# In the seven products of quadrants, VectorE's evacuations stand ahead of the weight splits of the same step

## The reference

```python
def swiglu_ffn(x, w_in, w_out):
    gate, up = jnp.split(x @ w_in, 2, axis=-1)
    return (jax.nn.silu(gate) * up) @ w_out
...
h = h + FFN_RES_WEIGHT * swiglu_ffn(rmsnorm(h, norm_ffn1[l]), ffn1_w_in[l], ffn1_w_out[l])
```

## Time and profile before

| | |
|---|---|
| median of 3 runs | 2157.2 us (2157.14 to 2157.84) |
| profiled execution, its own time | 2157.14 us |
| span of the profiled execution | 2155.3 us |
| TensorE busy | 2140.4 us, 99% of the span |
| VectorE busy | 1561.7 us, 72% |
| ScalarE busy | 891.9 us, 41% |
| granted TensorE clock, mean | 0.998 |

### The profile page before, as it was taken

The page is one execution under the profiler, slowest core; times in us unless marked ns, Lnnn a source line. Parts: engine busy times, 40 slices in busy tenths (PEclk is TensorE's granted clock), DMA queues, the critical chain, the costliest instruction groups (busy, mean ns, idle before and its releaser), DMA issues.

```text
span 2155.3 us, 30597 instructions
## 1 busy us (share of the span) xinstructions
PE 2140.4 (99%) x12718; PEld 1899.4 (88%) x12718; DVE 1561.7 (72%) x1798; ACT 891.9 (41%) x1110; POOL 166.0 (8%) x135
## 2 busy tenths in 40 slices
PE   9999999999999999999999999999999999999998
PEld 7998998888777888998998898998788888998997
DVE  8975976453466548984898897697788768874983
ACT  6532533242233425541445543344572356442443
POOL 0000003610123100000000000000102002000002
PEclk9999999999999999999999999999999999999999
DMA  4332332232222223332242233233222123332231
GB/s 162 108 128 69 108 118 98 98 118 95 81 79 78 80 88 116 108 128 78 99 134 84 79 106 127 79 99 108 88 69 69 50 86 111 99 127 79 98 132 45
DMA packets 59176, 210.39 MB, mean 98 GB/s; under 512 B 6560, under 2 KB 8992, under 8 KB 58784
## 3 DMA queue, kind: packets, MB, share of 16 engines
q1 hardware_dynamic: 58464, 205.30, 28.3%
q0 software_dynamic: 288, 2.62, 0.3%
q10 hardware_dynamic: 288, 0.52, 0.1%
HBM read 206.33 MB, written 2.10 MB: 97 GB/s over the span
## 4 chain that ended last, share of the span: by engine, by line
PE 94%; DVE 4%; ACT 1%; issue 1%; DMA 0%; SPq 0%; DVEq 0%; ACTq 0%
PE accs L672 25%; PE accs L673 25%; PE accs L674 25%; PE mixbs L674 3%; PE mixbs L673 3%; PE mixbs L672 3%; PE mixbs L1240 1%; PE mixbs L1217 1%; DVE w_lo L1834 1%; PE accs L1179 1%; PE accs L1178 1%; PE accs L1177 1%; ACT w_hi L1301 0%; PE mixbs L1059 0%; DVE rstd L1969 0%
## 5 line engine op out<-in xcount | busy, mean ns | idle before, releaser
L1301 ACT ACTIVATE w_hi<-w_raw 128x1024 fp32r<-128x1024 f32 x497 | 515.4, 1054 | 600.6 <-PE accs L674 281.9
L1834 DVE TENSOR_TENSOR w_lo<-w_raw,w_hi 128x1024 fp32r<-128x1024 f32 x497 | 613.7, 1238 | 108.9 <-ACT w_hi L1301 102.6
L672 PE MATMUL accs<-x_hi,w_hi 128*128 128x512 f32 (+1 forms) x1408 | 490.7, 349 | 2.1 <-DVE x_lo L1901 1.8
L674 PE MATMUL accs<-x_hi,w_lo 128*128 128x512 f32 (+1 forms) x1408 | 484.0, 344 | 0.0
L673 PE MATMUL accs<-x_lo,w_hi 128*128 128x512 f32 (+1 forms) x1408 | 483.8, 344 | 0.0
L672 PEld LDWEIGHTS accs<-x_hi,w_hi 128*128 128x128 f32 x1408 | 267.0, 190 | 35.6 <-DVE x_lo L1901 3.1
L674 PEld LDWEIGHTS accs<-x_hi,w_lo 128*128 128x128 f32 x1408 | 266.9, 190 | 32.0
L673 PEld LDWEIGHTS accs<-x_lo,w_hi 128*128 128x128 f32 x1408 | 267.2, 190 | 29.9
L672 PE MATMUL accs<-hid_hi,w_hi 128*128 128x512 f32 (+1 forms) x714 | 275.8, 386 | 0.0
L673 PE MATMUL accs<-hid_lo,w_hi 128*128 128x512 f32 (+1 forms) x714 | 275.7, 386 | 0.0
L674 PE MATMUL accs<-hid_hi,w_lo 128*128 128x512 f32 (+1 forms) x714 | 275.6, 386 | 0.0
(11 more groups left out here) (408 smaller groups left out, 3086.5 us busy)
## 6 DMA issues: line engine op xcount, KB each, us to landing
w_raw<-weights SPq DMA_DIRECT2D x383, 512.0 KB, 3.2
y_t<-h SPq DMA_DIRECT2D x16, 128.0 KB, 1.9
h<-x_t SPq DMA_DIRECT2D x3, 512.0 KB, 6.4
k1c<-const POOLq DMA_DIRECT2D x1, 1536.0 KB, 7.7
k2c<-const POOLq DMA_DIRECT2D x1, 1024.0 KB, 7.7
h<-x_t ACTq DMA_DIRECT2D x2, 256.0 KB, 4.0
w_raw<-weights SPq DMA_DIRECT2D x1, 384.0 KB, 4.8
cst<-const SPq DMA_DIRECT2D x1, 161.0 KB, 7.8
```

The lines of the kernel that those rows point to most:

```text
L672: pe.matmul(bank, w_hi[:, n % HI_SLOTS, w], hi, start=start, stop=False, skip_group_check=read_between)
L674: return pe.matmul(bank, w_lo[LO[n]][:, w], hi, start=False, stop=stop, skip_group_check=read_between)
L1301: act.activation(w_hi[:, n % HI_SLOTS, :], w_raw[RAW[n]][:, :], ACT.Copy).then_inc(hi_split, 1)
L1834: dve.tensor_tensor(w_lo[LO[n]][:, :], w_raw[RAW[n]][:, :], w_hi[:, n % HI_SLOTS, :].bitcast(F32), ALU.subtract).then_inc(lo_split, 1)
```

## The change

Four of the seven evacuations of a double are written ahead of the `prepare` that stood in front of them; the waits go with them. Nothing is added or removed. `prepare` brings the weight sum along where it has one (s3 with P3, s2 with block 7, the next P1).

```diff
                         dve.tensor_tensor(f_gate[:, :, t2], r_b, f_s[:, :, :], ALU.subtract).then_inc(quad, 1)
 
-                        prepare(n0 + P5)
                         dve.wait_ge(block_done, n0 + P2 + 1)
                         dve.tensor_tensor(f_gate[:, :, t1], r_a, rstd[:, :].unsqueeze(1).to_broadcast([P, 2, S])[:, :, t1],
                                           ALU.mult).then_inc(quad, 1)
-
-                        prepare(n0 + P4)
+                        prepare(n0 + P5)
+
                         dve.wait_ge(block_done, n0 + P7 + 1)
                         dve.tensor_tensor(f_up[:, :, t2], r_b, f_s[:, :, :], ALU.subtract).then_inc(quad, 1)
+                        prepare(n0 + P4)
                         if i:
                             hidden_rest(d - 1)
 
-                        prepare(n0 + P3)
                         dve.wait_ge(block_done, n0 + P5 + 1)
                         dve.wait_ge(quad, made(d, "u3"))
                         dve.tensor_tensor(f_up[:, :, t2], f_up[:, :, t2], r_c, ALU.subtract).then_inc(quad, 1)
-
-                        prepare(n0 + 7)
+                        prepare(n0 + P3)
+
                         dve.wait_ge(block_done, n0 + P4 + 1)
                         dve.tensor_tensor(f_up[:, :, t1], r_b, f_s[:, :, :], ALU.subtract).then_inc(quad, 1)
+                        prepare(n0 + 7)
 
                         prepare(n0 + 8)
```

## The result

The changed kernel takes 2181.48 us (median of 4 runs, 2181.30 to 2181.65) against 2157.21 us (4 runs): ratio 1.0112, 95% interval 1.0100 to 1.0124. It is 24.3 us slower. The forecast was 2180.2 us, range 2175 to 2187.

A forecast was written before the change was run, and what follows sets the result against it. TensorE was taken as the bound, with VectorE 19.25 of 20.16 us busy in a double; stalls of 0.44 and 0.33 us make +0.77 a round, 30 rounds 23.1 us on 2157.14, so 2180.2 us, range 2175 to 2187.

The forecast's parts named there:

- The two stalls: TensorE waits for late splits at P3, 0.44 us, and at P2', another 0.33 us, in each round.
- The pause ahead of L2104: VectorE's wait for P2 ahead of the first moved evacuation: 0.95 us, shrinking to 0.5 as VectorE is late.
- The 0.12 for ScalarE's rounding: At the split of P6': ScalarE rounds P6' only behind s2, so the split starts 0.12 us later.
- just in time: At P7': L2101 ends at 17.66, visible at 17.71, for a start of P7' at 17.73.
- the smallest is what decides: Before the change, splits were ready ahead of loads by 1.30 (P3), 1.31 (P1') and 0.48 us (P2'); the least decides.
- The price is that from here on VectorE is 1.13 us later: At L2110 ahead of the split of P4: that split now lies behind the wait for P7, delaying VectorE 1.13 us.
- The cover holds: Rival: VectorE's 19.28 us of work still fits a 20.16 us round, so not slower, 2157 us; chance 0.05.
- VectorE as the bound of a whole round: Rival: both VectorE pauses stay in full beside 19.28 us of work, +1.12 a round, 2190 us; chance 0.08.
- The clock: Rival: 60 new short stalls each cost TensorE the full clock for the next block, over 2330 us; chance 0.01.

The follow-up runs named there:

- third move alone: Kernel before with only L2117 put ahead of s3 and the split of P3, the split of P4 staying ahead of L2110: 2177.54 us, ratio 1.0093.
- fourth move alone: Kernel before with only L2121 put ahead of s2 and the split of P1': 2181.53 us, ratio 1.0111.
- second move alone: Kernel before with only L2110 put ahead of the split of P4: 2173.92 us, ratio 1.0076.
- first move: Kernel before with only L2105 put ahead of the split of P5: 2157.61 us against 2157.23, ratio 1.0001.
- P2' was cured: Full change with the hidden product L1980 put behind the split of P2' instead of ahead of it: 2179.54 us, ratio 1.0103.

## Why the prediction was right

**The total.** +0.77 us a round was forecast and +0.81 measured, in 30 rounds: 23.1 against 24.3 us.

**The two stalls.** P3's load was put at 5.88 and came at 5.89; P2's at 14.85 and came at 14.86. The pause ahead of L2104 was put at 0.47 (18.05 - 17.58 in the count of a late round, "0.5" in the rivals). That count sets VectorE free 0.60 us after L2101's start; counted alike it was 125.52 - (124.48 + 0.60) = 0.44. The 0.35 in the timeline counts from the end of L2101's record, 0.68 us after its start. The 0.12 for ScalarE's rounding was confirmed alone (0.13 to 0.15 by s2 ahead of L2120).

**The term that was short.** P7' was called "just in time" at 17.73. It came at 125.28 - 107.49 = 17.79. L2101 ended at 124.48 + 0.68 - 107.49 = 17.67, so the load came 0.12 later, not 0.05. The 0.05 was measured behind a split; behind L2101 it is 0.11 to 0.12 (more on that at the end). The prediction had allowed for 0.05 more at this place as a bound. This is the main part of the missing 0.04 a round.

**The block that decides.** The prediction compared the covers at P3, P1' and P2' and said of the 0.48 at P2' that "the smallest is what decides". It left P7' out of that comparison, whose first load waits for L2101. In the kernel before, L2101 ends at 121.61 + 0.68 - 105.88 = 16.41 and TensorE is ready for P7' at 16.96; with the 0.12 the cover is 0.43, less than that of P2'. In every slower kernel here P7' starts 0.11 to 0.12 us after L2101's end, whatever happened at P2'. With the third move alone L2101 ends 1.12 us later than before (103.58 + 0.68 - 86.73 = 17.53): 1.12 - 0.43 = 0.69, and P7' starts at 104.38 - 86.73 = 17.65, 0.69 late. In the change L2101 ends at 17.67, 1.26 later, and P7' starts at 17.79, 0.83 late. A round grows by some 0.02 us less than that, since the end of P7 follows its first load by about 3.18 us in these kernels and by 3.20 before. The forecast was this near because P2' and P7' almost tie: TensorE came from P2' only 0.05 us too early for P7'.

**The step whose wording was too narrow.** "The price is that from here on VectorE is 1.13 us later", said of L2110 and the split of P4, reads as if that move were the cause. The third and the fourth move alone, with that split where it was, cost 20.3 and 24.3 us. Three of the four moves each suffice, because each costs VectorE some 1.13 us ahead of a wait: the second puts one split behind it, and the third and the fourth leave VectorE with nothing to do from 1.74 to 2.88 and from 4.61 to 5.76. The cover takes off 0.43, and the second and third move alone measured 0.64 to 0.67 a round. The fourth has ScalarE's 0.15 on top. Together they cost no more than the worst of them, since the time lost ahead of one wait is not there to be lost ahead of the next.

**The rivals.** "The cover holds" was right for the first move and wrong for the rest. "VectorE as the bound of a whole round" has more in it than its chance of 0.08 says, since the stall moved from P2' to P7' when P2' was cured; but its price of +1.12 was too high, as the pause ahead of L2104 does shrink. The clock stayed at 1.00 through 60 stalls, in each of the 30 rounds, and in the mean of the span it is 0.998 in both kernels; the rule of the Trainium skill that was weighed there ("TensorE: Matmul & The Clock Gate", section "A second HAM failure mode: psum-queue depth-cycling") doesn't show itself in this kernel.

## What to carry to other kernels

On an engine that runs its program in order, a wait costs what could have been done ahead of it and is now behind it: write down, for every wait, what the engine has to do between it and each later deadline of the engine that bounds (here the evacuation that P7 needs, and not only the splits), and compare with the time between the two. A share of 72% over the span said nothing here; 19.25 of 20.16 us in the stretch said all. If results must be taken earlier, fill the time ahead of each wait with work of the same length that has no near deadline, and the earlier order is free.

## What the runs showed of the hardware that was not expected

The first weight load of a block starts 0.05 us after the end of a split that it waited for (113.38 against 112.11 + 1.22 in the changed kernel), but 0.11 to 0.12 us after the end of an evacuation: 92.39 against 91.60 + 0.68 with the second move alone, 125.28 against 124.48 + 0.68 in the change. That L2101 and L2117 read PSUM is not the reason. In the same changed kernel L2318 reads PSUM (`mixbs`) too, and the load that waits for it starts 0.05 us after its end, 621.92 + 0.68:

```profile
621.92 0.68 DVE L2318 TENSOR_TENSOR scored<-mixbs,k1c 128x512 f32<-128x512 f32 x1
...
622.65 0.19 PEld L1217 LDWEIGHTS mixbs<-qk 128*128 128x128 f32 x1
```

What goes with the longer time is where the wait stands. The wait for a split, and that for L2318, belongs to the weight load itself. P7 waits for two things, its split and L2101; the trace has the wait for L2101 as an instruction of its own in front of the load, one for each of the 38 doubles, 51 ns long (PEldq is the queue of the weight loads; the row gives least, median and longest in ns):

```profile
L760 PEldq EVENT_SEMAPHORE x38: 51/51/51, 62.3 to 2101.2; - x38
```

VectorE's L1923 shows both: at 21.65 + 0.69 with such an instruction in between, and the load at 22.45, 0.11 later; at 365.92 + 0.68 without one, and the load at 366.65, 0.05 later. No run changed this by itself.

And a block that starts after a stall is followed by the next 2.88 us later (113.38 to 116.26 in the change), so a stall of this size costs TensorE no more than its own length.
